# Wide products of the high and low rows of two mixer models, and their halves summed on VectorE

## The reference

```python
def mixer_block(h, ...):                       # first stack, both layers
    y_a, y_b, y_c = short_conv(...), retention(...), gated_linear_attention(...)
    merged = (sigmoid(gate_a) * (y_a @ w_branch_a) + sigmoid(gate_b) * (y_b @ w_branch_b)
              + sigmoid(gate_c) * (y_c @ w_branch_c))       # gates: columns of h @ w_in
    return merged @ w_out
def swiglu(h, w_gate, w_up, w_down):           # first stack, D_FF = 2816
    return (silu(h @ w_gate) * (h @ w_up)) @ w_down
# each layer: x = x + rms_norm(mixer(rms_norm(x))); x = x + rms_norm(swiglu(rms_norm(x)))

def conv_ffn(h, w_up, dw_w, dw_b, w_down):     # second stack, after its mixer and w_out
    u = dwconv(h @ w_up, dw_w, dw_b)           # width 3 along positions
    a, g = split(u, 2)
    return (a * silu(g)) @ w_down
```

## Time and profile before

| | |
|---|---|
| median of the three runs | 3028.82 us (3027.87 to 3029.64) |
| the profiled execution | 3016.1 us, of which its span, first to last instruction, is 3014.3 us |
| busy in the span | PE 94%, PEld 81%, POOL 50%, DVE 45%, ACT 44% |
| mean granted clock of TensorE | 0.973 of full speed |

### The profile page before, as it was taken

One profiled execution on the slowest core, in us unless ns is written; L12 is line 12 of the kernel. 1 busy time (PEld: TensorE's weight loads), 2 busy tenths in 40 slices (PEclk: granted clock), 3 DMA queues, 4 the chain that ended last, 5 costly groups with the idle time before them and its releaser, 6 DMA issues.

```text
span 3014.3 us, 44357 instructions
## 1 busy us (share of the span) xinstructions
PE 2825.6 (94%) x18084; PEld 2430.0 (81%) x18084; DVE 1349.9 (45%) x2106; ACT 1333.7 (44%) x2130; POOL 1505.3 (50%) x628
## 2 busy tenths in 40 slices
PE   7999999989999979989999989899998999998999
PEld 6889899888889977756777767688887868887999
DVE  5665411366551137943533432432335745446433
ACT  5464544545554443444233323342334554334554
POOL 4567578556757753311232324344444424445687
PEclk9999999999999999989999999999998989999999
DMA  5457775434777542211121213223332312223454
GB/s 189 133 191 244 236 235 192 133 119 158 260 247 252 176 133 84 77 35 36 53 67 49 84 50 98 70 96 101 98 98 93 106 47 98 88 95 119 147 182 161
DMA packets 144879, 386.60 MB, mean 128 GB/s; under 512 B 11824, under 2 KB 64304, under 8 KB 144688
## 3 DMA queue, kind: packets, MB, share of 16 engines
q1 hardware_dynamic: 144688, 383.87, 38.7%
HBM read 382.77 MB, written 1.05 MB: 127 GB/s over the span
## 4 chain that ended last, share of the span: by engine, by line
issue 35%; PE 32%; POOL 27%; DVE 4%; ACT 1%; POOLq 0%; DMA 0%; DVEq 0%; ACTq 0%
POOL w_lo L921 27%; PE bank L962 9%; PE bank L963 8%; PE bank L964 8%; PE bank L1309 1%; DVE sd L1715 1%; PE bank L1279 1%; PE bank L1028 1%; PE bank L995 1%; PE bank L1246 1%; PE bank L1231 1%; DVE bank L2094 0%; PE bank L984 0%; PE bank L983 0%; PE bank L982 0%
## 5 line engine op out<-in xcount | busy, mean ns | idle before, releaser
L921 POOL TENSOR_TENSOR w_lo<-raw,w_hi 128x1024 fp32r<-128x1024 f32 x624 | 1505.1, 2419 | 1498.0 <-ACT w_hi L1340 1497.0
L962 PE MATMUL bank<-h_hi,w_hi 128*128 128x256 f32 (+1 forms) x3456 | 1127.5, 326 | 78.8 <-DVE h_lo L2020 31.6
L963 PE MATMUL bank<-h_lo,w_hi 128*128 128x256 f32 (+1 forms) x3456 | 1097.9, 318 | 0.0
L964 PE MATMUL bank<-h_hi,w_lo 128*128 128x256 f32 (+1 forms) x3456 | 1097.2, 317 | 0.0
L1340 ACT ACTIVATE w_hi<-raw 128x1024 fp32r<-128x1024 f32 x624 | 655.2, 1054 | 398.8 <-PE bank L964 285.4
L962 PEld LDWEIGHTS bank<-h_hi,w_hi 128*128 128x128 f32 x3456 | 669.4, 194 | 172.8 <-issue 76.6
L963 PEld LDWEIGHTS bank<-h_lo,w_hi 128*128 128x128 f32 x3456 | 671.9, 194 | 42.6 <-issue 4.1
L964 PEld LDWEIGHTS bank<-h_hi,w_lo 128*128 128x128 f32 x3456 | 670.5, 194 | 40.7
L962 PE MATMUL bank<-hid_hi,w_hi 128*128 128x256 f32 (+1 forms) x704 | 218.2, 310 | 0.0
L963 PE MATMUL bank<-hid_lo,w_hi 128*128 128x256 f32 (+1 forms) x704 | 217.9, 309 | 0.0
L964 PE MATMUL bank<-hid_hi,w_lo 128*128 128x256 f32 (+1 forms) x704 | 217.9, 309 | 0.0
(11 more groups left out here) (273 smaller groups left out, 3522.2 us busy)
## 6 DMA issues: line engine op xcount, KB each, us to landing
raw<-stream SPq DMA_DIRECT2D x624, 512.0 KB, 3.4
spare_lo<-stream SPq DMA_DIRECT2D x32, 512.0 KB, 5.3
mix<-stream SPq DMA_DIRECT2D x32, 512.0 KB, 5.6
spare_hi<-stream SPq DMA_DIRECT2D x32, 512.0 KB, 5.7
xs<-x_rows SPq DMA_DIRECT2D x4, 256.0 KB, 4.1
xs<-ctx_rows SPq DMA_DIRECT2D x1, 1024.0 KB, 14.3
out_rows<-xs SPq DMA_DIRECT2D x8, 128.0 KB, 2.2
cst<-consts SPq DMA_DIRECT2D x1, 896.5 KB, 10.6
```

What stands on the lines that cost most here:

```text
L921: nc.gpsimd.tensor_tensor(w_lo[:, unit % SPLIT, :], raw[:, unit % RAW, :], w_hi[:, unit % SPLIT, :], ALU.subtract).then_inc(lo_ready, 1)
L962: nc.tensor.matmul(acc, wh, x_hi[:, k, c0:c1], start=k == 0, stop=False)
L963: nc.tensor.matmul(acc, wh, x_lo[:, k, c0:c1], start=False, stop=False)
L964: last = nc.tensor.matmul(acc, wl, x_hi[:, k, c0:c1], start=False, stop=k == t.k - 1)
```

## The change

`product_halves` replaces `product` for the first stack's gates and branches with b = 1 and 2, its FFN, and seven of the eight tiles each of its out and down products, and in the second stack's layer 1 for seven of the eight tiles of the out and down products and for all of the FFN's up products. For each block it issues one matmul of 512 columns, `w_hi` by the high and the low rows side by side (the two lie in one tensor now: `hl`, `y1`, `hid`, `hid2`), and one of 256 columns, `w_lo * x_hi`, into the first half of the bank. Within a unit the first wide one comes first if it opens the tile, then all low ones, then the wide ones. The second half of the bank holds `w_hi * x_lo`, so both halves have to be added: DVE does it, with a reduction over pairs (`add_halves`), and ACT works on the sum. The sum of a tile that is needed for one product only goes to the first half of bank 2 (`half_sum`). In the second stack's FFN the sums go to banks 4 and 5 to 7. `prod1`, `ff_u` and `ff_p` are gone. The tiles concerned take their banks from `THREE` (0, 1, 3). In `add_gated` two instructions add the two halves. The factor 0.5 of a branch moves into the split of the merged rows. The last tile of each out and down product stays narrow and is read as before.

```diff
+FEW, MANY, WITH_STAT, THREE = [0, 1], [0, 1, 3, 4, 5, 6, 7], [0, 1, 2], [0, 1, 3]
+SUM_A, SUMS_G = 4, [5, 6, 7]
...
+            if t.name in ("fa", "fg", "fd") and t.layer == DEPTH - 1:
+                pool = THREE
...
+            if t.name in ("ffg", "ffu") or t.array in ("w_branch_a", "w_branch_b", "w_branch_c") or (t.array, t.name) == ("w_in", "gate"):
+                pool = THREE
...
+    half_sum = STAT[:, 0:SEQ]
...
+            def product_halves(x, c0, c1, count=1, fresh=None, more=1):
+                for i_tile in range(count):
+                    t, n, b = TILES[at["tile"]], PLACE.first_out[at["tile"]], PLACE.first_block[at["tile"]]
+                    acc = bank_of(n)
+                    def high(k):
+                        w = w_hi[:, (b + k) // UNIT % SPLIT, (b + k) % UNIT * P:((b + k) % UNIT + 1) * P]
+                        return nc.tensor.matmul(acc[:, :], w, x[:, :, k, c0:c1], start=k == 0, stop=k == t.k - 1)
+                    def low(k):
+                        w = w_lo[:, (b + k) // UNIT % SPLIT, (b + k) % UNIT * P:((b + k) % UNIT + 1) * P]
+                        return nc.tensor.matmul(acc[:, 0:SEQ], w, x[:, 0, k, c0:c1], start=False, stop=False)
+                    k0 = 0
+                    while k0 < t.k:
+                        wait_unit((b + k0) // UNIT)
+                        k1 = min(t.k, k0 + (1 if fresh and i_tile == 0 else UNIT - (b + k0) % UNIT))
+                        if fresh and i_tile == 0:
+                            E.need(fresh, more)
+                        if k0 == 0:
+                            high(0)
+                        for k in range(k0, k1):
+                            last = low(k)
+                        for k in range(max(k0, 1), k1):
+                            last = high(k)
...
-                product(y1_hi, y1_lo, 0, SEQ, KD, fresh=merged_ready)
+                product_halves(y1, 0, SEQ, KD - 1, fresh=merged_ready)
+                product(y1, 0, SEQ)
...
+            def on_sum(rows, func, scale, done):          # ACT
+                n = next_tile()
+                E.later(tile_done, 1)
+                act.wait_ge(tile_out, n + 1)
+                nc.scalar.activation(rows, rows, func, scale=scale).then_inc(done, 1)
...
+            def add_halves(dst):                          # DVE
+                n = E.later(tile_out, 1) - 1
+                dve.wait_ge(tile_done, n + 1)
+                V.reduce_sum(dst, both_halves(banks[PLACE.bank[n]]), AX_X).then_inc(tile_out, 1)
+                return n + 1
...
             def add_normed(name, l):
-                E.later(tile_out, KD)
-                for k in range(KD - 1):
-                    add_square(k, c0, c1)
+                for f in range(KD - 1):
+                    add_halves(mix[:, f, c0:c1])
+                    if f >= 2:
+                        add_square(f - 2, c0, c1)
+                E.later(tile_out, 1)
+                add_square(KD - 3, c0, c1)
+                add_square(KD - 2, c0, c1)
...
                         else:
-                            V.scalar_tensor_tensor(p, g, 1.0, y, ADD, MUL).then_inc(merge_used, 1)
-                            dve.wait_ge(merge_used, 3 * KD * l + KD * b + f + 1)
-                            last = V.tensor_tensor(mix[:, f, SEQ:T2], mix[:, f, SEQ:T2], p, ADD)
+                            C.do(V.scalar_tensor_tensor(half_sum, g, 1.0, half_sum, ADD, MUL))
+                            C.settle()
+                            last = V.tensor_tensor(mix[:, f, SEQ:T2], mix[:, f, SEQ:T2], half_sum, ADD)
...
                             for j in range(2):
+                                    rows = banks[SUMS_G[t % len(SUMS_G)] if j else SUM_A][:, 0:SEQ]
+                                    n = E.later(tile_out, 1) - 1
+                                    dve.wait_ge(tile_done, n + 1)
+                                    C.do(V.reduce_sum(rows, both_halves(banks[PLACE.bank[n]]), AX_X))
+                                    C.settle()
+                                    dve.sem_inc(sum_ready, 1)
+                                    dve.sem_inc(tile_out, 1)
```

More of the change, by code:

```diff
@@ L636, in mixer_stack_kernel @@
     branch1 = r.put("branch1", [P, 2, SEQ])
-    prod1 = r.put("prod1", [P, 2, SEQ])
-    r.part(2 * 1024)
+    r.part(4 * 1024)
     o_sq = r.put("o_sq", [P, 2, 2 * SEQ])
@@ L944, in bank_of, with product @@
                 return banks[PLACE.bank[n]]
-            def product(x_hi, x_lo, c0, c1, count=1, fresh=None, late=None, more=1):
+            def product(x, c0, c1, count=1, fresh=None, late=None, more=1):
                 for i_tile in range(count):
@@ L1059, in _ @@
                         n = {"g": 5, "r": 2, "c": 3, "rg": RH, "gr": GH}[step]
-                        product(h_hi, h_lo, c0, c1, n, fresh=h_ready if step == "g" else None)
+                        product(hl, c0, c1, n, fresh=h_ready if step == "g" else None)
                     elif step in ("rv", "gv"):
@@ L1183, in _ @@
                         rows = slice(4 * b, 4 * b + 4) if b < 2 else slice(0, KD)
-                        product(y2_hi[:, rows, :], y2_lo[:, rows, :], c0, T2, late=late)
+                        product(y2[:, :, rows, :], c0, T2, late=late)
                     elif step == "qsum":
@@ L1525, in _ @@
                 merged(KD - 1)
-                take_rows(0, SEQ)
+                square_rows()
                 root(c0, c1, D)
@@ L2030, in add_gated @@
                     dve.wait_ge(tile_done, n + 1)
-                    for i in range(c0 // SEQ, 2):
-                        part = slice(i * SEQ, (i + 1) * SEQ)
-                        last = V.scalar_tensor_tensor(xs[:, f, part], banks[PLACE.bank[n]][:, part],
-                                                      mod[:, l, part_of_mod * KD + f, i:i + 1], xs[:, f, part], MUL, ADD)
+                    for i in range(1 if l == DEPTH - 1 and f == KD - 1 else 2):
+                        acc = slice(i * SEQ, (i + 1) * SEQ)
+                        if l == DEPTH - 1 and f == KD - 1:
+                            acc = slice(SEQ, T2)
+                        stream = i if l < DEPTH - 1 else 1
+                        part = slice(stream * SEQ, (stream + 1) * SEQ)
+                        last = V.scalar_tensor_tensor(xs[:, f, part], banks[PLACE.bank[n]][:, acc],
+                                                      mod[:, l, part_of_mod * KD + f, stream:stream + 1], xs[:, f, part], MUL, ADD)
+                        if l == DEPTH - 1 and i == 0 and f < KD - 1:
+                            C.do(last)
+                            C.settle()
                     last.then_inc(tile_out, 1)
@@ L2294, in _ @@
                             last.then_inc(fc_rows, 1)
-                            gate_bank.append(bank)
+                            gate_rows2.append(rows)
                         if 1 <= t <= FF_HALF:
```

222 lines of the change are left out of this document (133 added, 89 removed).

## The result

The changed kernel takes **3006.35 us** (median of 4 runs, 3005.28 to 3007.62); the kernel before, run beside it, 3029.23 us (3027.87 to 3032.65). The ratio is 0.9923, 95% interval 0.9906 to 0.994: 22.9 us faster, with 5 us either way. The profiled execution is one of these runs (3007.13 us).

A forecast was written before the change was run, and what follows sets the result against it. PE's instruction stream was taken to bound all changed stretches; -27.7 + 2.2 (post norms) + 1.0 (slipping steps) + 1.6 (ends of halves) = -22.9 us, from 3028.8 to 3005.9 us. The range was 2999 to 3034, the likeliest case 3000 to 3012.

The forecast's parts named there:

- The saving of the wide matmul: In all changed products, 2070 blocks each lose one instruction and 13.4 ns, 27.7 us less in all.
- a matmul costs its columns and 13.4 ns: On PE, 13.4 ns are left over beyond the columns at either width, taken as a matmul's price with its weight load.
- The bound from above (240 ns): On PE, the wide matmul costs at most 2 x 120.0 = 240 ns, at which nothing is saved.
- the rival without gain: In the wide products, a block still costs 360 ns and the ends cost 4.8 us: 3033.6 us, chance 0.10.
- the two runs of columns: In the wide matmul's rows, the 13.4 ns could belong to each run of columns read, two of 256, not the instruction.
- Gates and branches, "price: nothing": First stack, b = 1 and 2: DVE's 3.1 us a step fits within PE's 4.16 us, so no cost.
- The post norms: First stack after `w_out`: a reduction and three additions delay PE's row sum, 1.1 us a layer, 2.2 in all.
- The slipping loop: Second stack's FFN, layer 1: late steps add 1.0 us; as a rival, slower hand-overs give 3019 us, chance 0.14.
- The ends of the second stack's halves: Before the second stack's down products, PE waits for the last `hid2` rows: 1.6 us for both halves.
- The reduction: On DVE, adding a wide tile's halves takes 0.69 us; at 1.38 us, the slower rival gives 3044.5 us, chance 0.14.
- `add_gated`: Two instructions and a wait take 1.1 us a tile of at least 2.77 us, so they are hidden.
- the first stack's FFN: DVE needs some 2.3 us of PE's 5.55 us a step: no cost, and the stretch 4.7 us shorter a layer.

The follow-up runs named there:

- the run: The kernel before with only the first stack's gate and branch tiles moved to three PSUM banks instead of two, all products narrow: 3022.03 us, ratio 0.9987.
- the second profile: The changed kernel, unaltered, measured and profiled again on the same chip as the version with its additions moved: 3008.42 us, ratio to before 0.9947.

## Why the prediction came out right

3005.9 us was forecast and 3006.35 measured, but two of its terms were off by some 5 us each, in opposite directions, and the saving itself came out as 22.9 us in one measurement and 16.6 in another.

- **The saving of the wide matmul** was the right mechanism, 2070 blocks, with the wrong size: 10.6 ns, not 13.4, hence 22 us instead of 27.7. The step that failed is "a matmul costs its columns and 13.4 ns", read from stretches that had one width only. It holds in both of them, and not where the widths mix: there the wide matmul took 230 ns. The bound from above (240 ns) was far; the rival without gain was wrong, and so was the reason that I gave for doubt, the two runs of columns.
- The 2.5 ns that the Trainium skill gives as the fixed part of the gap of a warm matmul taken by itself (TensorE: Matmul & The Clock Gate, Back-to-back issue gap) would have made 2070 x 2.5 = an estimated 5.2 us. The trace does not agree: 10.6 ns a block.
- **Gates and branches, "price: nothing"** missed a gain. Three banks instead of two also serve the first branch, whose products stay narrow. I counted the waits of PE before the row sums and weights, but not those for a bank. It is worth 3 to 4 us by the run, about 5 by the stretches; both are rough.
- **The post norms** cost 1.6 and 1.4 us (1.35 each in the second profile) where 1.1 each stood. The place and the cause (additions with both inputs in SBUF, lengthened beside POOL) were as written. But 1.08 us is not what an addition costs: it is what one lasts that starts 1.61 us into POOL's instruction, as those of the earlier trace rows do. With the new order the starts moved, and one addition waited out a whole POOL instruction (2.65 us), which the prediction had as its bound.
- **The slipping loop** was put at 1.0 us and cost nothing: PE's idle time in the loop is zero, and the second half's up products take 61.47 us where they took 63.36, 176 x 10.7 ns less.
- **The ends of the second stack's halves**: its down products take 32.04 and 31.93 us, and 31.97 and 31.86 before, so the 77 x 10.6 ns = 0.8 us of each are lost. This makes 0.9 us a half (1.4 and 1.2 us in the second profile), 0.8 forecast. PE waits there for 0.49 and 0.48 us and takes the rows one at a time.
- **The reduction** at 0.69 us, `add_gated` and the first stack's FFN are as forecast.

Sum of the measured terms: -22.0 - 5 + 3.0 + 0 + 1.8 = -22.2 us, beside 22.9 and 16.6 in the medians and 19.3 in the table's stretches. The record doesn't say which of these is closest. So the direction and the mechanism were forecast; that the time is met within 0.5 us is luck.

## What to carry over

Read a rate in a stretch that has the mix of instructions which the change will make, or take it as a bound; a rate per width does not add up over widths. When a change touches the rotation of buffers, list who waited for a buffer before, also for the work that the change leaves as it is. And when an engine's list grows by a reduction a tile, move what doesn't depend on the last tile ahead of it: here that gave back 3 us for three lines. What such an instruction lasts beside another engine's depends on when it starts, so a duration read from the old order is a price for the old order only.

## What the hardware showed

A 512-column matmul started every 226.7 ns and a 256-column one every 120.0 ns when alone, at a granted clock of 1.00. In groups of eight of each they took 349.4 ns a pair instead of 346.7, with the first five wide ones 232 ns apart and the next three 227, and taken in turn 350 to 354 ns. Putting the rows side by side and cutting the DMA and POOL work to an eighth did not change that, and 512-column matmuls alone kept their 226.7 ns with and without shared weights. A reduction of pairs 256 elements apart in a bank took 0.69 us for 512 elements, as one in a row did. And an addition with two SBUF inputs that started during POOL's 2.4 us subtraction ended 0.28 to 0.29 us after it, 29 times of 29 in the kernel before: it lasted from 0.53 to 2.46 us there and up to 2.65 us in the changed kernel, where one that began within 0.01 us of POOL's start waited it out and another was through in 0.42 us. With the additions moved it took 0.88 us at the post norm. POOL's own 2.4 us did not change.
